# Head norms of the attention branch: the four sums of a batch go to four quarters of the array's columns, and the four roots are spread from four quarters of its rows

## What is computed

```python
q = (rms_norm(q_comp, q_a_norm) @ w_uq).reshape(B, S, MLA_HEADS, QK_NOPE + QK_ROPE)
kv = (rms_norm(kv_comp, kv_a_norm) @ w_ukv).reshape(B, S, MLA_HEADS, QK_NOPE + V_HEAD)
q_nope, q_pe = q[..., :QK_NOPE], q[..., QK_NOPE:]
...
q_nope = rms_norm(q_nope, q_norm_nope)
q_pe = apply_rope(rms_norm(q_pe, q_norm_rope), cos[:, :, None], sin[:, :, None])
k_nope = rms_norm(k_nope, k_norm_nope)
k_pe = apply_rope(rms_norm(k_rope_raw, k_norm_rope), cos, sin)
```

## Time and profile before

| | us |
|---|---|
| median of 3 runs | 2574.16 |
| lowest and highest | 2567.74, 2577.49 |
| the profiled execution | 2567.61 |
| its span, first to last instruction | 2565.9 |
| PE busy | 2471.4 (96%) |
| POOL busy | 1034.7 (40%) |
| DVE busy | 880.1 (34%) |
| ACT busy | 819.6 (32%) |
| granted PE clock, mean | 0.984 |

### The profile page before, as it was taken

The page is one execution under the profiler, slowest core; times in us unless marked ns, Lnnn a source line. Parts: engine busy times, 40 slices in busy tenths (PEclk is TensorE's granted clock), DMA queues, the critical chain, the costliest instruction groups (busy, mean ns, idle before and its releaser), DMA issues.

```text
span 2565.9 us, 28117 instructions
## 1 busy us (share of the span) xinstructions
PE 2471.4 (96%) x11092; PEld 1927.8 (75%) x11092; DVE 880.1 (34%) x1431; ACT 819.6 (32%) x1263; POOL 1034.7 (40%) x461
## 2 busy tenths in 40 slices
PE   6999999999999889999999999999999999999996
PEld 4676576677878778888778787878778788787885
DVE  4865346665120120040245443433421311201213
ACT  5243334334232222222334333333332311312232
POOL 1343222224465544444333333424334644445553
PEclk9999899999999989999999999999999999999998
DMA  8952133334344324333222232323233444444332
GB/s 306 404 200 70 37 104 112 124 114 144 101 142 144 120 92 136 95 99 99 75 74 77 72 99 83 106 80 116 85 104 95 140 148 127 132 151 132 91 98 83
DMA packets 97666, 308.40 MB, mean 120 GB/s; under 512 B 10488, under 2 KB 11768, under 8 KB 97408
## 3 DMA queue, kind: packets, MB, share of 16 engines
q1 hardware_dynamic: 97536, 306.62, 37.1%
HBM read 285.60 MB, written 20.97 MB: 119 GB/s over the span
## 4 chain that ended last, share of the span: by engine, by line
PE 82%; DVE 8%; DMA 4%; issue 3%; ACT 2%; POOL 1%; SPq 0%; DVEq 0%; ACTq 0%; POOLq 0%
PE bank L524 23%; PE bank L527 22%; PE bank L525 22%; DMA raw<-in_wst 3%; PE bank L520 2%; PE bank L521 2%; PE bank L523 2%; PE bank L1010 1%; PE bank L1034 1%; PE bank L1022 1%; DVE gac L1716 1%; PE bank L677 1%; PE bank L689 1%; PE bank L950 1%; DVE S L1995 1%
## 5 line engine op out<-in xcount | busy, mean ns | idle before, releaser
L2433 POOL TENSOR_TENSOR wlo<-raw,whi 128x1024 fp32r<-128x1024 f32 x356 | 869.8, 2448 | 1207.9 <-ACT whi L1125 1189.3
L524 PE MATMUL bank<-hhi,whi 128*128 128x512 f32 x2752 | 1092.4, 397 | 49.2 <-ACT whi L1125 26.1
L527 PE MATMUL bank<-hhi,wlo 128*128 128x512 f32 x2752 | 1081.5, 393 | 12.5 <-POOL wlo L2433 12.5
L525 PE MATMUL bank<-hlo,whi 128*128 128x512 f32 x2752 | 1078.6, 392 | 0.0
L524 PEld LDWEIGHTS bank<-hhi,whi 128*128 128x128 f32 x2752 | 520.1, 189 | 178.2 <-issue 31.9
L527 PEld LDWEIGHTS bank<-hhi,wlo 128*128 128x128 f32 x2752 | 519.8, 189 | 132.0 <-POOL wlo L2433 21.0
L525 PEld LDWEIGHTS bank<-hlo,whi 128*128 128x128 f32 x2752 | 520.3, 189 | 107.6 <-issue 1.4
L1125 ACT ACTIVATE whi<-raw 128x1024 fp32r<-128x1024 f32 x356 | 375.1, 1055 | 675.7 <-PE bank L527 468.5
L2255 DVE TENSOR_SCALAR S<-S,sm 128x512 f32<-128x512 f32 (+1 forms) x64 | 78.1, 1220 | 0.6
L520 PE MATMUL bank<-whi,hhi 128*128 128x512 f32 x192 | 75.0, 391 | 1.2 <-DVE HID L2146 1.2
L523 PE MATMUL bank<-wlo,hhi 128*128 128x512 f32 x192 | 74.7, 389 | 0.0
(11 more groups left out here) (313 smaller groups left out, 2209.9 us busy)
## 6 DMA issues: line engine op xcount, KB each, us to landing
raw<-in_wst SPq DMA_DIRECT2D x407, 512.0 KB, 3.6
rawx<-in_wst SPq DMA_DIRECT2D x54, 512.0 KB, 8.4
rawy<-in_wst SPq DMA_DIRECT2D x24, 512.0 KB, 5.9
tgs<-TS SPq DMA_DIRECT2D x32, 256.0 KB, 3.9
axr<-tgs SPq DMA_DIRECT2D x32, 256.0 KB, 4.0
X<-in_xt SPq DMA_DIRECT2D x4, 1024.0 KB, 14.7
pls<-stg SPq DMA_DIRECT2D x16, 256.0 KB, 9.5
axr<-in_xt SPq DMA_DIRECT2D x16, 256.0 KB, 2.8
```

The costliest lines, as they stand in the source:

```text
L524: e.matmul(o, hi, xh, start=first, stop=False)
L525: e.matmul(o, hi, xl, start=False, stop=False)
L527: return e.matmul(o, lo, xh, start=False, stop=last)
L2433: e.tensor_tensor(sub(wlo, PAIR[c], CH), slots[slot(c)], sub(whi, PAIR[c], CH).bitcast(F), ALU.subtract).then_inc(*up("wlo_pool", "wlo", c))
```

## The change

The sums: each of the four matmuls has 32 columns of weights (32 ones, or for the rotary batches 16 for each 64 features) and writes 32 rows of the bank: tile `b` the rows 32b to 32b+31. Each is a sum of its own and nothing accumulates. All four `nsq` are waited for before the first matmul. Roots and reciprocals are then of 128x512 (32x512 for `kr`).

The spread: matmul `b` reads rows 32b to 32b+31 of `nrs` and of `SELB`, which has a one in row 32b (and in row 32b+16 for the second head of a rotary tile). The four of a batch, or two and two for `qr`, are issued in a row. All the banks they go to are claimed and waited for before the first of them. For `qr` both tiles of a pair are scaled by DVE in a row before the rotation of the first. `SELB` is 128x256 instead of 8x1024.

```diff
-                rows_ = 8 if rope else 4
                 o, prior = claim(ring("side"), "nsum", key)
...
                 for b in range(blocks):
-                    sel = C("sr")[:, 8 * b:8 * b + 8] if rope else C("sn")[:, 4 * b:4 * b + 4]
                     w.wait_ge(*done("nsq", key, b))
+                for b in range(blocks):
                     src = krs if key == "kr" else nsq[b]
-                    e.matmul(o[0:rows_, :], sel, src[:, :], start=b == 0, stop=b == blocks - 1).then_inc(
-                        *up("stat_pe", "nsum", key, b))
+                    e.matmul(o[32 * b:32 * b + 32, :], C("sr") if rope else C("ones")[:, 0:32], src[:, :],
+                             start=True, stop=True).then_inc(*up("stat_pe", "nsum", key, b))
                 yield
                 if rope:
                     yield
-                for b in range(blocks):
-                    o, prior = claim(ring("side"), "nbc", key, b)
+
+                def spread(some):
+
+                    to = [claim(ring("side"), "nbc", key, b) for b in some]
                     w.wait_ge(*done("nrs", key))
                     w.wait_ge("selb", 16)
-                    for f in prior:
-                        w.wait_ge(*f)
-                    ri = NRI[key]
-                    e.matmul(o[:, :], SELB[0:rows_, 512 * rope + P * b:512 * rope + P * (b + 1)],
-                             nrs[ri][0:rows_, :], start=True, stop=True).then_inc(*up("stat_pe", "nbc", key, b))
-                    if not rope:
-                        continue
+                    for o, prior in to:
+                        for f in prior:
+                            w.wait_ge(*f)
+                    for b, (o, prior) in zip(some, to):
+                        e.matmul(o[:, :], SELB[32 * b:32 * b + 32, P * rope:P * rope + P],
+                                 nrs[NRI[key]][32 * b:32 * b + 32, :], start=True, stop=True).then_inc(
+                            *up("stat_pe", "nbc", key, b))
+
+                if not rope:
+                    spread(range(4))
+                    return
+                for b in range(blocks):
+                    if b % 2 == 0:
+                        spread(range(b, min(b + 2, blocks)))
                     yield
                     o, prior = claim(ring("side"), "rot", key, b)
...
-                rows_ = 8 if rope else 4
+                rows_ = 32 if key == "kr" else P
...
+                for b, (dst, gain) in enumerate(blocks):
...
+                    if b % 2 == 0:
+                        for d in range(b, min(b + 2, len(blocks))):
+                            scaled_rope(d)
+                    yield
...
-            e.dma_start(SELB[0:8, :], selb).then_inc(*up("selb", by=16))
+            e.dma_start(SELB[:, :], selb).then_inc(*up("selb", by=16))
```

More of the change, by code:

```diff
@@ L39 @@
 for _n, _w in [("ident", 128), ("ones", 128), ("bd", 128), ("perm", 128), ("t0", 512), ("t1", 512),
-               ("tc", 4 * NC), ("mc", NC), ("sn", 16), ("sr", 32), ("s32", 1)]:
+               ("tc", 4 * NC), ("mc", NC), ("sr", 32), ("s32", 1)]:
     CST[_n] = (_at, _at + _w)
@@ L368, in build @@
         krs = area(44, 1, "krs")
-        SELB = area(96, 1, "SELB", F, 1024)
+        SELB = area(96, 1, "SELB", F, 256)
         nsq = [area(2 * i, 1, f"nsq{i}") for i in range(4)]
@@ L1906, in norm_batch, with scaled_rope @@
                     yield
-                for b, (dst, gain) in enumerate(blocks):
+                def scaled_rope(b):
+                    dst, gain = blocks[b]
                     o = bank("nbc", key, b)
@@ L1910, in norm_batch @@
                     w.wait_ge(*done("raw", key, b))
[L1911 to L1914, removed]
                     xn = nxn[b % 2][:, :]
@@ L1924, in norm_batch @@
                         *up("norm_dve", "nxn", key, b, frees=("nbc", key, b)))
+                for b, (dst, gain) in enumerate(blocks):
+                    if not rope:
+                        o = bank("nbc", key, b)
+                        w.wait_ge(*done("nbc", key, b))
+                        w.wait_ge(*done("raw", key, b))
+                        e.scalar_tensor_tensor(dst, dst, gain, o[:, :], ALU.mult, ALU.mult).then_inc(
+                            *up("norm_dve", "head", key, b, frees=("nbc", key, b)))
+                        continue
+                    if b % 2 == 0:
+                        for d in range(b, min(b + 2, len(blocks))):
+                            scaled_rope(d)
                     yield
+                    xn = nxn[b % 2][:, :]
                     o = bank("rot", key, b)
@@ L2802, in _constants @@
     put("mc", dc[:, 0] >= 0)
[L2804 to L2810, removed]
+    put("sr", (p // 64) == (np.arange(32)[None] // 16))
     put("s32", p % 32 == 0)
@@ L2815, in _selectors @@
 def _selectors():
[L2817 to L2822, removed]
+    out = np.zeros((4, 32, 2, P), np.float32)
+    out[:, 0, 0] = 1.0
+    out[:, 0, 1, 0:64] = 1.0
+    out[:, 16, 1, 64:128] = 1.0
+    return out.reshape(P, 2 * P)
 def kernel(**inputs):
```

## The result

The changed kernel takes **2544.45 us** (median of 4 runs, 2543.70 to 2549.48) against 2572.68 us for the kernel before (4 runs, 2567.74 to 2577.49). The ratio of the two is 0.9887, with a 95% interval of 0.9862 to 0.9912: 1.1% faster, a small gain but clear of no change. The forecast was 2549, with a range of 2538 to 2562, and faster as the likeliest case. The profiled execution of the changed kernel took 2543.70 us (span 2542.0, mean granted clock 0.985), that of the kernel before 2567.61: 23.9 us less.

The account below looks back on a forecast made before the run. PE was taken as the bound, holding 82% of the chain that ended last. The pieces of the head norms summed to -25.4 us, carried whole to the end: 2574.16 - 25.4 = 2548.8, rounded to 2549, range 2538 to 2562.

Parts of the forecast that it names:

- 230.28, first pair, rotations, sums of `q0`: Stretch of 7.60 us: packed spreads 1.05, wait 0.8 for `nxn`, rotation 1.05, sums 1.0; with +0.2, -3.5 us.
- 243.54, second pair and spreads of `q0`: Stretch of 5.35 us: all four spreads wait for bank 3 until DVE's `nxn` at 249.24, +1.45 us.
- 248.89, dense: Dense chunk of 7.25 us at clock 0.76 behind the `q0` spreads: left at 0, between -1.55 and +3.
- 256.14, rotations and sums of `q1`: Stretch of 11.27 us: both rotations in a row 1.75, sums 1.0, 0.1 between, so -8.4 us.
- 277.13, dense: Dense chunk behind the spreads of `q1`: 8.44 to 5.7 us as the run of spreads in front shortens, -2.7.
- What a packed group costs: Four sums in column quarters 1.0 us; four spreads in row quarters 1.05, between bounds of 1.0 and 1.9.
- half packed rivals: Column weight loads stand alone (3.5 us) or row quarters run as two pairs (3.4): -22, both -18.5; chance 0.08.
- The added wait: At 243.54, `q0`'s spreads wait for bank 3 until DVE scales `qr` tile 2; about 4 us idle, +1.45.
- The rival that the low clock moves: Clock falls as often as now around idle and thin work in the norms: change -18, at 2556; chance 0.17.
- The 1.3 us for the last square: Before the sums of `k0` and `k1`, PE waits for ACT's squares, 1.3 us each; both sums together -2.4.
- The 0.2 for the reciprocal: Before `q1`'s spreads: reciprocal done at 8.3, PE there at 8.4; 0.2 us of wait taken, leaving -2.8.
- the rival in which the gain is lost behind: After the norms, something in attention is set by time, not PE: up to 15 us return, 2560 to 2574; chance 0.08.

Follow-up runs that it names:

- The deferred pair: The changed kernel with the second pair of rotary spreads of `qr` one chunk later, behind the fourth `uq` chunk: 2541.26 us, ratio 0.9863.
- the longest execution: The kernel before, unedited, profiled again in four more executions; the longest of them took 2583.88 us.

## Why the prediction was right, and where it was off

The steps of the sum beside what the trace of the changed kernel has, in us:

| piece | predicted | measured |
|---|---|---|
| sums of `qr` | -2.5 | -2.5 |
| 230.28, first pair, rotations, sums of `q0` | -3.5 | -3.6 |
| 243.54, second pair and spreads of `q0` | +1.45 | +2.7 |
| 248.89, dense | 0 | -0.05 |
| 256.14, rotations and sums of `q1` | -8.4 | -8.5 |
| spreads of `q1` | -2.8 | -2.95 |
| 277.13, dense | -2.7 | -2.7 |
| sums of `k0` and `k1` | -2.4 | -2.5 |
| spreads of `k0` | -2.6 | -2.6 |
| spreads of `k1` | -1.9 | -2.35 |
| together | -25.4 | -25.1 |

**What a packed group costs.** The two nearest rows carried this. Column quarters were put at 1.0 from the earlier trace rows and took 1.00. Row quarters into four banks had no row; they were put at 1.05 between 1.0 and 1.9, and took 1.07. Both half packed rivals fall: the eight loads of the column quarters take 0.16 us together,

```profile
214.33 0.16 PEld L676 LDWEIGHTS bank<-nsq,ct 128*32 128x32 f32 x8 [0.76 <-ACT nsq L1310]
...
L676 PEld LDWEIGHTS bank<-nsq,ct x40: 106/107/109, 214.3 to 283.8; 128*32 128x32 f32 x40
```

and those of the row quarters 0.31. One load of the sums takes 0.107 us, so eight in turn would take 0.86. So the loads for different columns of the same rows don't stand in turn. They lie within the first matmul, which takes 0.59 us. The rule of the Trainium skill ("TensorE: Matmul & The Clock Gate", Part 3), by which a weight load overlaps a running matmul only where its row group differs, would have had them wait; here the measurement decides against it. The same Part also lets loads into a background weight buffer go ahead, which the prediction left out. The same page's 3.07 for four tiles of 32 rows gave an estimated 1.1 us, which agrees with 1.07.

**The added wait** was found in the right place, with the right cause: PE's spreads of `q0` behind DVE's `nxn`, behind the slow add. They started 6.00 us after the end of the chunk, where the working has 249.3 - 243.54 = 5.8. The size of the piece was off by 1.2: I had costed the four spreads at 1.05, and they took 2.02 because the clock was already down when they began. I had foreseen the fall and left it all to the dense piece behind. The +2.7 lies within the bounds of both pieces together.

**The low clock.** Of the three places before, those around 256 and 277 are gone, as forecast, and one is left at `q0`, behind the idle stretch. The rival that the low clock moves (-18) is not what happened: idle of 1.27 us at `k0` was followed by a clock of 1.00. That idleness brings the throttle back is what the Trainium skill says (same page, Part 1), and the one place at which PE had several idle microseconds agrees. The deferred pair, which takes the idle away, takes the low clock with it. For the three places before, the runs show that the low clock went, and not which part of the change took it away.

**Waits.** The 1.3 us for the last square at `k0` and `k1` came as worked out (1.27). The 0.2 for the reciprocal before `q1`'s spreads was not there on PE: the row at 260.91 has it for the loads, which come early, but not for the matmul. It was as close as the working says: the reciprocal ends at 260.86, 8.46 us after the end of the chunk, and PE is there at 8.51. At `k1` the spreads did not wait for ACT's bank, and about 0.2 us are lost to DVE behind them (16.67 us from the chunk behind them to the first score, against 16.47), instead of 0.2 + 0.4.

**Rows and reciprocals.** The reciprocal on 128 rows takes what it took on 4, 3.34 us in the earlier trace rows:

```profile
257.51 3.35 DVE L1911 RECIPROCAL nrs<-nrs 128x512 f32<-128x512 f32 x1
```

**Behind the norms.** I carried the whole shift to the end. The first score comes 25.1 us earlier, the end of the profiled execution 23.9: about 1.2 us come back later. In which wait was not looked for by a run, so this stays open; it is small against the up to 15 us of the rival in which the gain is lost behind.

**The median** came out 4.5 us below the forecast of 2549, although the sum was 1.5 too large for the profiles. The step that was off is the last one: I set the shift of one execution against the median of three, as if all executions of the kernel before lost the same to the clock. They don't: the medians moved by 28.2 us where the profiles moved by 23.9. Of the 4.5 us, 1.5 are the base alone, whose median went from 2574.16 to 2572.68 with a fourth run. The two errors also work against each other, which is luck: with the 23.9 us of the profiles in place of 25.4 the forecast would have been 2550.

## What to carry to other kernels

Small fp32 matmuls that stand in a row, of up to 32 columns or 32 rows each, cost as much as full ones when they go one after another, and about a third when four go to four quarters: 1.0 instead of 3.5 us here, for columns and rows alike. A packed group takes the latest of its inputs and of its banks' readers as its start, so look in the order at which member arrives last, and put that member in another gap: 3.9 us of idle cost 6.4 here, with the clock. And where a kernel's runs lie further apart than its changes, read the clock of several executions before a median is taken as the base of a sum.

## What the hardware showed that I had not expected

- Loads for four quarters of the columns, all to the same 128 rows, take 0.16 us for eight, while a single one of them takes 0.107.
- The clock fell during PE's idle stretch of 3.92 us (mean 0.83 in it), and the half clock then held for the spreads (2.09 us instead of 1.14) and part of the next chunk (0.76).
- Matmuls of 4 rows were followed by a clock of 0.65 behind the spreads of `q1`, those of 128 rows there by 1.00, in both kernels that had them. Behind the spreads of `k0`, also of 4 rows, it was 1.00 in the first profile and 0.77 in the longest execution. So the same instructions come out either way, and thin rows alone don't decide it; what does stays open.
- DVE's operation with both inputs in SBUF takes 2.81 us instead of 0.69 when it begins just behind a POOL operation of 2.34 us, as `tensor_tensor` and as `scalar_tensor_tensor`; one that reads a bank ran in 0.63 beside POOL.
